# Three moves around the first expert job of a two-layer decoder kernel: the last slab's transposes, GpSimd's row multiplication, and the routing exponentials

## The reference, cut to what matters

```python
logits = jnp.einsum('bsd,de->bse', h, router_w)          # h = rms_norm(x), 8 experts
top_val, top_idx = lax.top_k(logits, 2)
gates = jax.nn.softmax(top_val, axis=-1)
for e in range(8):
    out = out + gate[..., e:e+1] * ((silu(h @ wg[e]) * (h @ wu[e])) @ wd[e])   # hidden width 3584
x = x + out
```

## Time and profile before

| | |
|---|---|
| median of three runs (lowest, highest) | 1378.92 us (1378.88, 1379.09) |
| the profiled execution | 1378.75 us |
| its span, first to last instruction | 1376.8 us |
| TensorE busy | 1357.4 us (99%) |
| VectorE busy | 1182.4 us (86%) |
| ScalarE busy | 1021.3 us (74%) |
| GpSimd busy | 123.7 us (9%) |
| mean granted TensorE clock | 0.999 |

### The profile page before, as it was taken

The page is one execution under the profiler, slowest core; times in us unless marked ns, Lnnn a source line. Parts: engine busy times, 40 slices in busy tenths (PEclk is TensorE's granted clock), DMA queues, the critical chain, the costliest instruction groups (busy, mean ns, idle before and its releaser), DMA issues.

```text
span 1376.8 us, 19928 instructions
## 1 busy us (share of the span) xinstructions
PE 1357.4 (99%) x6885; PEld 1139.8 (83%) x6885; DVE 1182.4 (86%) x1393; ACT 1021.3 (74%) x1213; POOL 123.7 (9%) x132
## 2 busy tenths in 40 slices
PE   9999999999999999999999999999999999999998
PEld 7778999988887788888888888888888888888886
DVE  5876655568959999999999999999999999999998
ACT  5666444466757788888888888888888888888886
POOL 1020000000331220100200100020020002003000
PEclk9999999999999999999999999999999999999999
DMA  9944543633667999999999999999999999999980
GB/s 347 361 151 151 184 153 123 244 124 123 246 238 275 357 387 352 394 392 372 364 393 386 354 391 396 369 365 394 385 353 391 393 370 366 393 382 352 394 323 31
DMA packets 184623, 430.88 MB, mean 313 GB/s; under 512 B 6076, under 2 KB 14032, under 8 KB 184576
## 3 DMA queue, kind: packets, MB, share of 16 engines
q1 hardware_dynamic: 181136, 422.81, 82.7%
q0 software_dynamic: 3440, 7.44, 2.6%
HBM read 425.68 MB, written 7.36 MB: 315 GB/s over the span
## 4 chain that ended last, share of the span: by engine, by line
PE 89%; DVE 8%; issue 1%; ACT 1%; DVEq 0%; ACTq 0%
PE psum L786 28%; PE psum L788 28%; PE psum L787 28%; DVE w_lo L428 3%; PE psum L1356 1%; DVE w_lo L410 1%; DVE moe_h L2464 0%; DVE moe_hT_lo L2455 0%; PE psum L818 0%; PE psum L919 0%; PE psum L1217 0%; DVE probs L2109 0%; PE psum L1060 0%; PE psum L951 0%; PE psum L1227 0%
## 5 line engine op out<-in xcount | busy, mean ns | idle before, releaser
L428 DVE TENSOR_TENSOR w_lo<-raw_ring,w_hi 128x1024 fp32r<-128x1024 f32 x674 | 810.6, 1223 | 55.4 <-ACT w_hi L423 11.2
L423 ACT ACTIVATE w_hi<-raw_ring 128x1024 fp32r<-128x1024 f32 x675 | 714.3, 1062 | 168.1 <-PE psum L788 168.0
L786 PE MATMUL psum<-w_hi,xg_hi 128*128 128x512 f32 x896 | 353.6, 395 | 0.7 <-DVE w_lo L428 0.7
L788 PE MATMUL psum<-w_hi,xg_lo 128*128 128x512 f32 x896 | 349.5, 390 | 0.0
L787 PE MATMUL psum<-w_lo,xg_hi 128*128 128x512 f32 x896 | 349.0, 389 | 0.0
L410 DVE TENSOR_TENSOR w_lo<-raw_ring,w_hi 128x1024 fp32r<-128x1024 f32 x124 | 151.3, 1227 | 77.9 <-ACT w_hi L402 77.0
L402 ACT ACTIVATE w_hi<-raw_ring 128x1024 fp32r<-128x1024 f32 x124 | 130.1, 1057 | 94.0 <-PE psum L788 93.7
L788 PEld LDWEIGHTS psum<-w_hi,xg_lo 128*128 128x128 f32 x896 | 168.1, 188 | 35.7
L786 PEld LDWEIGHTS psum<-w_hi,xg_hi 128*128 128x128 f32 x896 | 168.4, 188 | 35.0 <-issue 1.3
L787 PEld LDWEIGHTS psum<-w_lo,xg_hi 128*128 128x128 f32 x896 | 168.5, 188 | 33.7
L786 PE MATMUL psum<-w_hi,moe_hT_hi 128*128 128x512 f32 x448 | 176.0, 393 | 3.4 <-DVE moe_hT_lo L2455 3.4
(11 more groups left out here) (299 smaller groups left out, 1357.1 us busy)
## 6 DMA issues: line engine op xcount, KB each, us to landing
raw_ring<-in_moe_w_gate SPq DMA_DIRECT2D x56, 2048.0 KB, 10.6
raw_ring<-in_moe_w_up SPq DMA_DIRECT2D x56, 2048.0 KB, 10.3
raw_ring<-in_moe_w_down SPq DMA_DIRECT2D x56, 2048.0 KB, 10.6
raw_ring<-in_ffn_w_gate SPq DMA_DIRECT2D x5, 2048.0 KB, 8.2
raw_ring<-in_ffn_w_up SPq DMA_DIRECT2D x5, 2048.0 KB, 12.0
raw_ring<-in_ffn_w_down SPq DMA_DIRECT2D x5, 2048.0 KB, 10.3
raw_ring<-in_w_in_ab SPq DMA_DIRECT2D x4, 2048.0 KB, 16.0
raw_ring<-in_w_in_cd SPq DMA_DIRECT2D x4, 2048.0 KB, 8.8
```

The source lines that it names most:

```text
L423: act.activation(wh[:, v % SPLITS, :], moe_raw(i, q), ACT.Copy).then_inc(hi_ready, 1)
L428: dve.tensor_tensor(wl[:, v % SPLITS, :], moe_raw(i, q), wh[:, v % SPLITS, :].bitcast(F32), ALU.subtract).then_inc(lo_ready, 1)
L786: pe.matmul(out_, sh, mh_, start=start, stop=False)
L788: return pe.matmul(out_, sl, mh_, start=False, stop=stop)
```

## The change

Five edits in three places.

1. TensorE transposes the last slab behind the first unit of step d5 instead of the second; ScalarE and VectorE do its turned_h one unit earlier in their split loops. The place of gate_times_up isn't changed.
2. GpSimd waits for xg_lo_ready = 2 ahead of the first multiplication.
3. On VectorE positions(1), the split of unit 1 and the threshold now stand ahead of the maxima and their difference; on ScalarE the exponentials stand behind first_gathered.

```diff
@@ GpSimd
             pool.wait_ge(row_gain_loaded, 16)
+            pool.wait_ge(xg_lo_ready, 2)
             for t in range(TT):
                 pool.wait_ge(xs_rows_ready, t + 1)
@@ TensorE
-                        if kind == "d" and i == SLABS - 2 and q == 1:
+                        if kind == "d" and i == SLABS - 2 and q == 0:
                             transpose_h(j, SLABS - 1)
@@ ScalarE
+            first_gathered()
             act.wait_ge(diff_ready, 1)
             for t in range(TT):
                 ins = act.activation(rt[:, T_EXP + t:T_EXP + t + 1], rt[:, T_DIFF + t:T_DIFF + t + 1], ACT.Exp,
                                      scale=small[:, RS + t:RS + t + 1])
             ins.then_inc(exp_ready, 1)
-            first_gathered()
             act.preload_act_table(ACT.Silu)
...
-                        if kind == "d" and i == SLABS - 2 and w == 4 * v + SPLITS + 2:
+                        if kind == "d" and i == SLABS - 2 and w == 4 * v + SPLITS + 1:
                             turned_h(j, SLABS - 1)
@@ VectorE
             ranks(1)
+            positions(1)
+            moe_split_lo(dve, 0, 1)
+            dve.tensor_scalar(r(T_OVER, NE), ps[:, 5, TT * NE:TT * NE + NE], P + 0.5, None, ALU.is_gt)
             for t in range(TT):
                 ins = dve.max(r(T_MX + t * NE, NE), r(T_LG + t * NE, NE))
...
-            positions(1)
...
-            dve.tensor_scalar(r(T_OVER, NE), ps[:, 5, TT * NE:TT * NE + NE], P + 0.5, None, ALU.is_gt)
-            moe_split_lo(dve, 0, 1)
             first_gathered()
...
-                        if kind == "d" and i == SLABS - 2 and w == 4 * v + SPLITS + 2:
+                        if kind == "d" and i == SLABS - 2 and w == 4 * v + SPLITS + 1:
                             turned_h(j, SLABS - 1)
```

## The result

The kernel after takes 1383.17 us (median of nine runs, 1382.69 to 1383.40), the kernel before in the same sessions 1379.09 us (nine runs, 1377.96 to 1379.63). The ratio is 1.0030 with a 95% interval of 1.0021 to 1.0039: **slower by 4.1 us**, clear of what the measurement can tell. The forecast was 1383.6 us, which is +4.7 us on the 1378.92 us that it started from.

The account below looks back on a forecast made before the run. TensorE was taken as the bound, holding 89% of the chain of waits. 1378.75 + 3.6 (last slab) + 1.1 (way into job 0 with multiplications), and 0.17 against the median, gave 1383.6 us; range 1379.0 to 1386.0.

Parts of the forecast that it names:

- Part 1: Last slab's transposes one unit earlier: TensorE waits for moe_h in each job; +0.45 us a job, +3.6 us in all.
- Part 2: Way into job 0: second gather starts at 415.8 at full clock, third unit at 420.85; gain 2.85 us.
- Part 3: Job 0: each GpSimd multiplication holds one VectorE split, making the fifth unit late; +1.1 us including Part 2's gain.
- the rival with a falling clock: TensorE's clock falls in the new stalls on the way into job 0: up to 1385.3 us; chance 0.13.
- bound for one hold: Way into job 0, only one held split that counts: -1.1 us for Part 2 and Part 3 together.
- The sum: Whole kernel: 1378.75 + 3.6 + 1.1 us, and 0.17 more against the median, giving 1383.6 us.
- That splits aren't held: Job 0: GpSimd's multiplications don't delay VectorE's splits, so -2.85 us there; 1379.7 us in all; chance 0.2.
- The faster rival: Step d5: moe_h ready before the first unit ends, 0.73 us wait gone in eight jobs; 1374.2 us; chance 0.07.

Follow-up runs that it names:

- e1: The kernel before with only the last slab's transposes and both turned_h one unit earlier: 1382.12 us, ratio 1.0024.
- e4: The kernel before with only GpSimd's wait for xg_lo_ready = 2 added: 1380.23 us, ratio 1.0009.
- e3: The kernel before with only the new order on VectorE and ScalarE, without GpSimd's wait or the slab move: 1377.87 us, ratio 0.9995.
- e9: The kernel before with only gate_times_up of the last slab one split earlier, transposes at their old place: 1379.07 us, ratio 1.0002.
- e2: The kernel after with the slab move undone, keeping the new order and GpSimd's wait: 1379.82 us, ratio 1.0008.
- e6: The kernel after with GpSimd's second multiplication done once more: 1385.31 us, ratio 1.0044 against the kernel before.
- e5: The kernel after with gate_times_up of the last slab one split earlier on VectorE: 1374.33 us, ratio 0.9964 against the kernel before.
- e8: The kernel after with the last slab's gate_times_up one split earlier and, replacing GpSimd's xg_lo wait, only the second multiplication waiting for the difference: 1370.80 us, ratio 0.9937.

## Why the prediction was right

**Part 1** held in its mechanism: moe_h didn't come earlier, TensorE waits for it in all eight jobs, and d6 is free. It was forecast at +0.45 us a job, +3.6 in all; the trace shows 0.40 and 3.2, and e1 +3.3. The idle time was taken as 1.13 us and up to 0.1 for the start; it is 1.09 with the start in it, since the signal from moe_h takes 0.06 us (651.48 to 651.54), not the 0.12 of moe_hT_lo.

**Part 2** held: the gather starts at 416.78 - 0.96 = 415.82 (forecast 415.8) at full clock, and the third unit at 420.76 (420.85). But the part credits this to both edits. Its sentence that after the change neither the multiplication nor the maxima stand ahead of pick is true of the program; as a cause only the first half counts, as e4 and e3 show. It also takes the half clock of the one profiled execution as what every execution pays. By the trace of e9, without the fall, the gain up to the third unit would be 1.65 us instead of 2.94 (7.73 us behind the last count there, 6.08 in the kernel after).

**Part 3** held as well: both splits at 3.4 us, as forecast, and the fifth unit 0.8 us late instead of 1.1. The missing 0.3 us lies ahead of the multiplications: VectorE begins the split of unit 2 at 420.23 - 0.96 = 419.27, not at 419.6. The two idle times are 1.58 and 1.66 us in the brackets, against 1.9 forecast; a bracket starts only at the end of the last matmul's record, and from start to start units 3 and 4 lose 1.77 and 1.96 us. The clock stayed at 1.00, so the rival with a falling clock didn't occur. The part's bound for one hold, -1.1, comes out at -0.9 by its own times; nothing rests on it.

**The sum** was 0.6 us above the measured change (+4.7 and +4.1), and some of this closeness is luck. The forecast compares with an execution that had the fall at the gather. Against one without it, as in e9, the traces give 8 x 0.40 + 2.07 = 5.3 us (the fifth unit 12.53 and 10.46 us behind the last count). The measured 4.1 compares with a median over executions that seem to be of both kinds, and e2's +1.0 lies between 0.79 and 2.07 for the same reason, as far as the traces tell.

**The rivals.** That splits aren't held is refuted by the rows of the kernel after and by e6. The faster rival named its point rightly, moe_h earlier by 1.0 us: e5 moves it by one split, and the outcome is on the other side, at 1374.33 us where this rival had 1374.2. As a forecast of this change it was wrong, since nothing in the diff moves moe_h.

## What to carry to other kernels

When a consumer is moved forward in one engine's program, look up when its input is produced on the other engine. If that is less ahead than the move is long, the producer has to move too: here one line turned +3.3 us into -5.8. And a large GpSimd operation belongs beside VectorE work that reads PSUM (here 2.38 us beside it, against 3.25 and 3.35 beside splits); a wait that moves it out of one critical stretch can put it into the next. Last, a single profiled execution can hold a cost that others don't have, as the half clock at the gather here.

## What the runs showed of the hardware

- Beside a GpSimd tensor_tensor of 128 x 1024, a VectorE operation with two SBUF inputs waits until it is over (3.4 instead of 1.2 us), and so does a small one with its single input in SBUF (1.56 instead of 0.17 us, e3). Those with one input from PSUM aren't held: 0.17 us in e3, 2.16 us for eight in e8. That the single SBUF input is enough was not expected. It isn't enough in every row: two maxima of 128 x 8 with a single SBUF input, just behind the listed start of the multiplication in the kernel before (414.35), take 0.24 us together, as in e4 with GpSimd idle beside them. Whether such an operation isn't held, or the hold begins a little after the listed start, no run separates. The row, from the kernel before:

```profile
414.44 0.24 DVE L2419 MAX8 routing<-routing 128x8 f32<-128x8 f32 x2
```

- The two engines took turns: in the kernel after and in e6 GpSimd got in behind every single split, though VectorE had the next one ready, and VectorE behind every multiplication.
- TensorE's clock fell to 1.2 GHz at the gather behind an idle time of 2.07 us in the kernel before, of 2.06 us in e1 (0.50 in 419.00 to 422.20) and of 1.79 us in e3 (0.51 in 418.30 to 421.60). It stayed at 2.4 GHz at the same gather behind the same 2.07 us in e9, and behind 1.58 and 1.66 us in the kernel after, where TensorE had done a full unit ahead of them. So the length of the idle time by itself doesn't decide; what does is open.
